# Two engines for the input squares, a diagonal product in place of scaled transposes, and another order of the first loads, in a hybrid attention, convolution and expert block on one Trainium2 core

## What is computed

```python
def rmsnorm(x, g):
    y = x * lax.rsqrt(jnp.mean(x * x, axis=-1, keepdims=True) + EPS)
    return y * g

h = rmsnorm(x, g_mix)
proj = h @ w_in              # (512, 1024) @ (1024, 5120): q | k | v | GLU input | gates
...                          # differential attention, causal depthwise convolution, merge,
...                          # output product, residual
x = x + hier_moe(rmsnorm(x, g_ffn), ...)     # 64 experts in 8 groups, top 2 of one group
out = rmsnorm(x, g_final)
```

## Time and profile before

| | us |
|---|---|
| median of 3 runs | 1398.61 |
| the three runs | 1397.33, 1398.61, 1398.95 |
| the profiled execution, its own time | 1396.9 |
| its span | 1395.1 |
| TensorE busy in it | 1324.5 |
| VectorE busy in it | 432.3 |
| ScalarE busy in it | 209.3 |
| GpSimd busy in it | 186.1 |

### The profile page before, as it was taken

The page is one execution under the profiler, slowest core; times in us unless marked ns, Lnnn a source line. Parts: engine busy times, 40 slices in busy tenths (PEclk is TensorE's granted clock), DMA queues, the critical chain, the costliest instruction groups (busy, mean ns, idle before and its releaser), DMA issues.

```text
span 1395.1 us, 17476 instructions
## 1 busy us (share of the span) xinstructions
PE 1324.5 (95%) x5883; PEld 577.4 (41%) x5883; DVE 432.3 (31%) x843; ACT 209.3 (15%) x453; POOL 186.1 (13%) x244
## 2 busy tenths in 40 slices
PE   5999988999979999999999999999999999999991
PEld 3878766744443333333333333333333333333330
DVE  4799354342243211221221121122122112112214
ACT  3133324430110000000100100000010010000002
POOL 2355343000000010010001001001000100100100
PEclk9999999999989999999999999999999999999996
DMA  5331311125146999999999999999999999999984
GB/s 208 112 125 61 121 61 47 53 82 226 75 181 240 396 416 416 418 417 416 417 418 416 416 417 416 415 417 417 416 417 415 413 414 415 411 416 417 413 343 187
DMA packets 93090, 435.78 MB, mean 312 GB/s; under 512 B 13488, under 2 KB 13517, under 8 KB 60810
## 3 DMA queue, kind: packets, MB, share of 16 engines
q1 hardware_dynamic: 86896, 429.23, 76.3%
q0 software_dynamic: 5312, 5.28, 1.1%
q10 hardware_dynamic: 858, 0.95, 0.2%
HBM read 429.10 MB, written 18.36 MB: 321 GB/s over the span
## 4 chain that ended last, share of the span: by engine, by line
issue 78%; PE 13%; POOL 2%; DVE 2%; DMA 2%; POOLq 1%; ACT 1%; ACTq 0%; DVEq 0%
PE ps_proj L1193 10%; PE ps_proj L1234 2%; POOL sb_tick L578 1%; POOL sb_tick L589 1%; DVE sb_x L1142 1%; DMA sb_weights<-in_w_in 1%; DMA sb_rb_sb<-in_rel_bias 1%; PE ps_scores L1248 1%; POOL expert_rows L579 0%; DVE sb_x L1152 0%; DVE sb_conv L932 0%; DMA sb_weights<-expert_rows 0%; POOL sb_weights_r L557 0%; PE ps_proj L1225 0%; POOLq L596 0%
## 5 line engine op out<-in xcount | busy, mean ns | idle before, releaser
L1405 PE MATMUL ps_proj<-sb_weights,sb_scratch 128*64 128x512 f32 x1984 | 446.9, 593 | 0.8 <-DVE sb_scratch L1107 0.8
L1405 PEld LDWEIGHTS ps_proj<-sb_weights,sb_scratch 128*64 128x64 f32 x1984 | 142.7, 137 | 282.9 <-issue 270.5
L1382 PE MATMUL ps_proj<-sb_hT,sb_scratch 128*64 128x512 f32 x1008 | 253.6, 604 | 0.0
L1426 PE MATMUL ps_scores<-sb_weights,sb_scratch 128*64 128x512 f32 x992 | 237.1, 599 | 0.0
L1117 DVE TENSOR_TENSOR sb_scratch<-sb_scratch,ps_proj 128x256 f32<-128x256 f32 x62 | 26.1, 421 | 535.9 <-ACT sb_scratch L765 535.9
L578 POOL TENSOR_TENSOR sb_tick<-sb_tick 1x1 f32<-1x1 f32 x62 | 11.6, 187 | 1009.5 <-ACT sb_scratch L773 1009.5
L1193 PE MATMUL ps_proj<-sb_hT_r,sb_weights_r 128*128 128x512 f32 x512 | 128.3, 405 | 2.7 <-POOL sb_weights_r L557 2.7
L1382 PEld LDWEIGHTS ps_proj<-sb_hT,sb_scratch 128*64 128x64 f32 x1008 | 67.4, 138 | 120.2 <-issue 120.2
L1426 PEld LDWEIGHTS ps_scores<-sb_weights,sb_scratch 128*64 128x64 f32 x992 | 65.4, 136 | 116.8 <-issue 91.2
L1193 PEld LDWEIGHTS ps_proj<-sb_hT_r,sb_weights_r 128*128 128x128 f32 x512 | 97.9, 194 | 30.9 <-issue 10.2
L765 ACT ACTIVATE sb_scratch<-ps_proj 128x256 f32<-128x256 f32 x62 | 23.8, 383 | 491.6 <-PE ps_proj L1405 491.6
(11 more groups left out here) (221 smaller groups left out, 803.3 us busy)
## 6 DMA issues: line engine op xcount, KB each, us to landing
sb_weights<-in_w_exp_down SPq DMA_DIRECT2D x124, 1024.0 KB, 14.6
sb_weights<-in_w_exp_gate SPq DMA_DIRECT2D x124, 1024.0 KB, 14.5
sb_weights<-in_w_exp_up SPq DMA_DIRECT2D x124, 1024.0 KB, 15.2
sb_weights<-in_w_in SPq DMA_DIRECT2D x9, 2048.0 KB, 8.0
sb_x<-in_x SPq DMA_DIRECT2D x8, 512.0 KB, 9.0
sb_weights<-in_w_out SPq DMA_DIRECT2D x2, 2048.0 KB, 10.7
sb_weights<-expert_rows SPq DMA_DIRECT2D x4, 1024.0 KB, 7.9
sb_weights<-in_w_conv_pw SPq DMA_DIRECT2D x1, 2048.0 KB, 7.7
```

Of the source, the lines that this page charges most:

```text
L1382: last = mm(ps_rows[g * BLK:(g + 1) * BLK, :], onehot[:, t, :], h2[:, t, g * NW:(g + 1) * NW], start=t == 0, stop=t == T - 1)
L1405: last = mm(ps_gu[g * BLK:(g + 1) * BLK, :].rearrange("p (a n) -> p a n", a=2), hTb[:, c, half * BLK:(half + 1) * BLK], weights[:, place(p ...
L1426: last = mm(ps_y[g * BLK:(g + 1) * BLK, :], actT[:, j, half * BLK:(half + 1) * BLK], weights[:, place(parity, 4 + half), 2 * j + g, :], st ...
```

## The change

- x is loaded into `x_in`, which is the area where `xn` was. The squares' junk output goes to `x`.
- VectorE squares tiles 0 and 2, ScalarE tiles 1 and 3 (Square with scale D^-0.5). ScalarE runs one root on a constant first, before x is there.
- VectorE makes no scaled copy. For each token tile it multiplies the identity with the column of reciprocals: a 128x128 diagonal, `rstd_diag`.
- TensorE makes, for each 128x128 block, a product of x_in with the diagonal in place of the transpose of the scaled copy. It waits for all four diagonals.
- The constants are loaded in two parts: the identity (128 columns) first in ScalarE's queue, the rest behind the small vectors, the taps and the bias table. TensorE's first instruction waits for both.
- SP no longer waits ahead of the first weights.
- The high part of the first weight piece stands behind the third "xT" copy of ScalarE, not the sixth.

```diff
-        xn = dense[:, 0:T * D].rearrange("p (t d) -> p t d", t=T)
+        x_in = dense[:, 0:T * D].rearrange("p (t d) -> p t d", t=T)
+        rstd_diag = scratch[:, 2048:2048 + T * P].rearrange("p (t q) -> p t q", q=P)
...
@@ block.sync
             for t in range(T):
-                sp.dma_start(x[:, t, :], ap("x")[0, t * P:(t + 1) * P, :]).then_inc(in_x[t], 16)
-            sp.wait_ge(in_const, 16)
-            sp.wait_ge(in_small, 16 * (len(VEC_ROWS) + 2))
+                sp.dma_start(x_in[:, t, :], ap("x")[0, t * P:(t + 1) * P, :]).then_inc(in_x[t], 16)
...
@@ block.scalar
-            act_e.dma_start(consts[:, :], ap("consts")).then_inc(in_const, 16)
+            act_e.dma_start(consts[:, 0:P], ap("consts")[:, 0:P]).then_inc(in_const, 16)
...
             act_e.dma_start(taps_row[:, :], ap("w_dw")[0]).then_inc(in_small, 16)
             act_e.dma_start(rb_sb[:, :], ap("rel_bias")).then_inc(in_small, 16)
+            act_e.dma_start(consts[:, P:], ap("consts")[:, P:]).then_inc(in_const2, 16)
...
             act_e.wait_ge(eps_set, 1)
+            act_e.activation(rms[:, 0:1], eps_col, ACT.Sqrt, bias=eps_col).then_inc(table_set, 1)
+            act_e.wait_ge(table_set, 1)
             for t in range(T):
-                act_e.wait_ge(x_sq, t + 1)
+                if t % 2 == 0:
+                    act_e.wait_ge(in_x[t + 1], 16)
+                    act_e.activation(x[:, t + 1, :], x_in[:, t + 1, :], ACT.Square, scale=D ** -0.5,
+                                     accum_out=ssq[:, t + 1:t + 2]).then_inc(x_sq_s, 1)
+                    act_e.wait_ge(x_sq, t // 2 + 1)
+                else:
+                    act_e.wait_ge(x_sq_s, t // 2 + 1)
                 act_e.activation(rms[:, t:t + 1], ssq[:, t:t + 1], ACT.Sqrt, bias=eps_col).then_inc(x_rms, 1)
...
-                if c == 5:
+                if c == 2:
                     high_part(0)
...
@@ block.vector
-                dve.tensor_tensor_reduce(out=xn[:, t, :], in0=x[:, t, :], in1=x[:, t, :], scale=1.0 / D, scalar=0.0,
+                dve.tensor_tensor_reduce(out=x[:, t, :], in0=x_in[:, t, :], in1=x_in[:, t, :], scale=1.0 / D, scalar=0.0,
...
-            def scale_x(t):
+            def diag_x(t):
                 dve.wait_ge(x_rms, t + 1)
                 link(dve.reciprocal(rstd[:, t:t + 1], rms[:, t:t + 1]))
-                dve.tensor_scalar(xn[:, t, :], x[:, t, :], rstd[:, t:t + 1], None, ALU.mult).then_inc(xn_ready, 1)
+                dve.tensor_scalar(rstd_diag[:, t, :], ident, rstd[:, t:t + 1], None, ALU.mult).then_inc(diag_ready, 1)
 
             square_x(0)
-            for t in range(1, T):
-                square_x(t)
-                scale_x(t - 1)
-            scale_x(T - 1)
+            square_x(2)
+            dve.wait_ge(in_const, 16)
+            for t in range(T):
+                diag_x(t)
...
@@ block.tensor
             pe.wait_ge(in_const, 16)
+            pe.wait_ge(in_const2, 16)
             pe.wait_ge(in_small, 16 * (len(VEC_ROWS) + 2))
...
-            pe.wait_ge(xn_ready, T)
+            pe.wait_ge(diag_ready, T)
             for c in range(KD):
                 dst = open_tile("xT", c)
                 for t in range(T):
-                    last = pe.transpose(dst[:, t * P:(t + 1) * P], xn[:, t, c * P:(c + 1) * P], ident)
+                    last = mm(dst[:, t * P:(t + 1) * P], x_in[:, t, c * P:(c + 1) * P], rstd_diag[:, t, :], start=True, stop=True)
                 last.then_inc(tile_done, 1)
```

More of the change, by code:

```diff
@@ L317, in block_kernel @@
         ps_y, ps_slots = ps_s[:, 0, :], ps_s[:, 1, :]
-        in_const, in_small, in_bcast = sem("in_const"), sem("in_small"), sem("in_bcast")
+        in_const, in_const2, in_small, in_bcast = sem("in_const"), sem("in_const2"), sem("in_small"), sem("in_bcast")
         in_x = [sem(f"in_x{t}") for t in range(T)]
@@ L330, in block_kernel @@
         link_s = sem("link_s")
-        x_sq, x_rms, xn_ready = sem("x_sq"), sem("x_rms"), sem("xn_ready")
+        x_sq, x_sq_s, x_rms, diag_ready, table_set = sem("x_sq"), sem("x_sq_s"), sem("x_rms"), sem("diag_ready"), sem("table_set")
         tick_set = sem("tick_set")
```

## The result

The changed kernel is **slower**: 1401.82 us (median of 8 runs, 1400.50 to 1402.81) against 1397.41 of the kernel before (median of 8, the three of the table before among them). The ratio is 1.0033, 95% interval 1.0024 to 1.0042. The profiled execution took 1402.22 us, its span is 1400.3, 5.2 more than the span before.

The account below looks back on a forecast made before the run. TensorE, busy 95% of the span, bounds the kernel; a chain of waits from the bias table's load sets the first 30 us. +1.4 + 1.5 - 1.8 = +1.1 on a 1398.61 median gave 1399.7, range 1396.2 to 1402.8.

Parts of the forecast that it names:

- A: The forecast case for the whole kernel: +1.1 us, 1399.7 us; chance 0.48.
- Rival C: ScalarE's queue, one DMA engine: remaining constants arrive last, TensorE starts at up to 17.4, +3.8 us, 1402.4; chance 0.12.
- step (4): Stage of x on TensorE: products in place of transposes delay the first weights to 28.5 us, +1.5 (bounds +0.9, +2.4).
- Step (1): Norm work on VectorE and ScalarE: squares on two engines are worth 0, covered by some 3 us.
- Step (2): SP's queue: weights issued first land near 18 us; alone worth nearly 0, at best 0.5 us.
- Step (3): DMA queues taking turns: taps and constants wait for weight packets, TensorE starts at 14.7 instead of 13.27, +1.4 us.
- The estimate of 21 turns: Identity and vector rows ahead of the taps on their DMA engine: about 21 turns of 0.18, from 2.4 to 6.2 us.
- Step (5): TensorE's clock at the first weight piece: stays up after a 1.8 us pause instead of 2.7, -1.8 us.
- B: TensorE's clock falls all the same after the shorter pause: +2.9 us, 1401.5; chance 0.24.
- Rival E: Stage of x on TensorE: a product costs four transposes, not two, 7 us later, 1406.7; chance 0.02.

Follow-up runs that it names:

- b_weights_first: The kernel before with only SP's wait ahead of the first weights removed; ratio to the kernel before 1.0007 (0.9998 to 1.0017).
- best_prod_long: best_prod with 48 idle products instead of 40; ratio to the kernel before 0.9981 (0.9972 to 0.9991).
- best_transp: Changed kernel with taps in two loads, transposes for products, 40 idle products, 16 idle transposes, first weights' high part behind fifth copy; 1393.09 us, ratio 0.9968.
- a_transposes: Changed kernel with transposes in place of the products, VectorE scaling x in place; ratio to the kernel before 1.0014 (1.0004 to 1.0023).
- a_taps_transp: Changed kernel with tap rows in two loads and transposes in place of the products; ratio to the kernel before 0.9988 (0.9978 to 0.9997).
- best_prod: best_transp with the changed kernel's diagonal products in place of the transposes; ratio to the kernel before 0.9976 (0.9967 to 0.9986).

## Why the prediction was right and where it was wrong

What was right is the way the start hangs together: which load TensorE would wait for, that the squares are worth nothing, and that the shorter pause saves the clock. The size was not. I forecast +1.1 us and measured +4.4. The whole interval of the ratio lies beyond the 0.2% up to which I spoke of no change (0.65); "slower by over 0.2%" is what happened, and I had given it 0.28. The median, 1401.82, lies inside the range, but that is luck of the base: the forecast stood on 1398.61, the median of three runs, where eight gave 1397.41. By the ratio on the forecast's base (1398.61 x 1.0033 = 1403.2) it would lie 0.4 above the range. My likeliest case (A, 1399.7, +1.1) did not happen. **Rival C did**, the constants arriving last of all: I had put its threshold at a landing after 16.4, its worst price at +3.8, and its chance at 0.12; they landed at 16.46 and the kernel lost 4.4. The late start was less than C's worst (+3.28 against +4.1); with the products at my price it would have come to +3.1. The rest is step (4).

- **Step (1)**, squares worth 0 and covered by 3 us: right. The cover was 7 us. The 128x128 scaling, priced at 0.29, took 0.29.
- **Step (2)**, early weights worth nearly 0: right as a gain. They landed at 18.7 (issued at 2.7, 16.0 us to landing) where I had said near 18. b_weights_first shows that they also cost 1.55 us.
- **Step (3)** is the step that failed first: right in mechanism, mis-sized, +1.4 forecast and **+3.28** measured. By the trace's packets the taps ran from 8.2 to 13.4, one each 0.16 us, and the constants on that engine from 13.8 to 15.9. I had the two rates nearly right (0.165 for a tap with its neighbour, 2.3 us for the constants, which took 2.15), but let the taps begin at 6.2. The last of the small rows ahead of them went out at 7.8. The estimate of 21 turns ahead of them was 2 us short, and from the last packet to TensorE's start it took 0.6 us and not 0.3. In the kernel before, too, the first tap row went out only at 7.9 by the packets of its trace; so the start could have been read and not estimated. x left the engines at 9.0 and not by 8, as I had said against C. The middle of the bounds was the wrong value to take; the row with its 9.18 us from issue to landing, for a load that had no weights against it, should have pulled it up.
- **Step (4)**, +1.5 forecast and **+2.80** measured. The price per instruction was nearly right cold (0.23 forecast, 0.21 measured) and right with the clock up (0.11). I let the clock come up at about 20; it came up near 24, 7.5 us after TensorE's first instruction, so that 22 product instructions ran cold and not ten. In the kernel before the rise had come 6.3 us after it, which from a start at 14.7 would have made it 21, an estimate from that one trace. My bound with the clock 2 us later was +2.4. With the clock up the products cost 0.9 (best_prod_long against best_transp).
- **Step (5)**, the clock stays up after the shorter pause: right, -1.64. It was not due to the products: a_transposes has it too. The pause became shorter because the high part of the first piece moved forward: the pause ended with VectorE's last low part (1.87 us in the changed kernel and in a_transposes), where in b_weights_first it ended with GpSimd's split (2.95 us). That is read from who released TensorE; no run moves the high part alone. a_taps_transp, in which the clock fell after the same pause, says that B deserved the chance that I gave it.
- That the shift carries through to the end unchanged: right within the 1360.3 to 1363.5 of the table. Rival E, four transposes for a product, is out: 64 instructions did the work, at the transposes' pace each.

## What to carry to other kernels

A small load counts by the engine that it passes and by what stands ahead of it, not by its bytes: before big loads are issued early, look which small ones the first instruction waits for, and cut a load whose rows all pass a single engine (31 rows did, 16 and 15 did not). An instruction count doubled on TensorE for eight tiles cost 0.9 us while the clock was up and 3.1 at this kernel's start. Where elementwise work ends 4 us before the load that TensorE waits for, making it shorter brings nothing until the load is mended.

## What the runs showed of the hardware that was not expected

- 31 rows of 2 KB in one load, against 16 and 15 rows in two: 12.09 and 7.64 us from issue to landing of the load behind them.
- TensorE's clock came up 6.3 to 8.8 us after its first real instruction when it had been idle before (nine kernels), and 3.4 to 5.9 us after the first of a stretch of idle products (five). Among the instructions that ran as it came up were FP32 transposes: in a_taps_transp TensorE had done nothing else for 5.8 us.
- A pause of 1.9 us ahead of the first piece lowered it in one kernel of five, and it fell in best_prod after one of 0.8 us ahead of the small work, where best_prod_long, without that pause, kept it up. What decides stays open.
- 16 idle transposes in a 2.7 us pause made the kernel faster by 0.23% (0.13 to 0.34%).
